# A hybrid decoder step on one core: sample attention started two pairs earlier, both lead-ins reordered, out-projection products moved ahead of the last values

## What is computed

```python
# layer 0: h @ w_in -> q, k, v, xq
o  = softmax(q k^T * hd**-0.5 - slopes*dist, with a sink per head) v   # window 128, 12 heads, 4 kv heads
xo = softmax(xq mk^T * hd**-0.5) mv                                    # 4 heads into 256 memory tokens
x  = x + concat([o, xo]) @ w_out
# layer 1: o = u * (tril(W_s) v_norm + b) in chunks of 128; xo and x as in layer 0
# samples: the same with cached keys and values, 8 batches of 4 tokens
```

## Time and profile before

| | us |
|---|---|
| median of 3 runs | 2238.39 (2238.03 to 2239.85) |
| the profiled execution | 2238.22 |
| its span, first to last instruction | 2236.3 |
| PE busy in the span | 2216.7 |
| DVE, ACT, POOL busy | 1174.1, 664.5, 553.2 |
| mean granted TensorE clock | 0.999 of full speed |

### The profile page before, as it was taken

The page is one execution under the profiler, slowest core; times in us unless marked ns, Lnnn a source line. Parts: engine busy times, 40 slices in busy tenths (PEclk is TensorE's granted clock), DMA queues, the critical chain, the costliest instruction groups (busy, mean ns, idle before and its releaser), DMA issues.

```text
span 2236.3 us, 39236 instructions
## 1 busy us (share of the span) xinstructions
PE 2216.7 (99%) x15320; PEld 2142.0 (96%) x15320; DVE 1174.1 (53%) x2164; ACT 664.5 (30%) x1208; POOL 553.2 (25%) x422
## 2 busy tenths in 40 slices
PE   9999999999999999999999999999999999999999
PEld 8997689999999999999999997999999999999999
DVE  8355761745545455444575256165545455454554
ACT  6314962512221122221253226142221122221121
POOL 0004634312221122221252223332221122221221
PEclk9999999999999999999999999999999999999999
DMA  5223001111111011110111130111111111110112
GB/s 189 82 97 141 13 18 43 57 39 47 56 56 34 32 47 56 56 38 29 49 49 61 47 109 18 47 38 57 57 49 37 37 47 56 56 38 28 47 57 91
DMA packets 39305, 123.43 MB, mean 55 GB/s; under 512 B 5328, under 2 KB 13488, under 8 KB 38416
## 3 DMA queue, kind: packets, MB, share of 16 engines
q1 hardware_dynamic: 36384, 113.25, 15.3%
q10 hardware_dynamic: 2832, 8.94, 1.1%
HBM read 115.57 MB, written 8.63 MB: 56 GB/s over the span
## 4 chain that ended last, share of the span: by engine, by line
PE 93%; DVE 3%; ACT 2%; issue 1%; POOL 1%; DMA 0%; SPq 0%; DVEq 0%; ACTq 0%; POOLq 0%
PE ps L634 29%; PE ps L635 29%; PE ps L636 29%; DVE h_lo L1743 2%; ACT s_exp L1437 1%; PE ps L982 1%; PE ps L1027 1%; PE ps L1008 1%; PE ps L815 1%; PE ps L951 1%; ACT p_t L1222 0%; PE ps L803 0%; PE ps L770 0%; DMA x<-in_x_t 0%; PE ps L954 0%
## 5 line engine op out<-in xcount | busy, mean ns | idle before, releaser
L634 PE MATMUL ps<-h_hi,w_hi 128*128 128x352 f32 x3120 | 1013.3, 325 | 4.6 <-DVE h_lo L1743 4.4
L635 PE MATMUL ps<-h_lo,w_hi 128*128 128x352 f32 x3120 | 1000.9, 321 | 0.0
L636 PE MATMUL ps<-h_hi,w_lo 128*128 128x352 f32 x3120 | 1000.4, 321 | 0.0
L486 POOL TENSOR_TENSOR w_lo<-raw,w_hi 128x1024 fp32r<-128x1024 f32 x118 | 298.5, 2530 | 1497.0 <-ACT w_hi L1222 1497.0
L634 PEld LDWEIGHTS ps<-h_hi,w_hi 128*128 128x128 f32 x3120 | 585.8, 188 | 17.2 <-issue 6.2
L635 PEld LDWEIGHTS ps<-h_lo,w_hi 128*128 128x128 f32 x3120 | 586.9, 188 | 0.7
L636 PEld LDWEIGHTS ps<-h_hi,w_lo 128*128 128x128 f32 x3120 | 585.4, 188 | 0.0
L2160 DVE TENSOR_TENSOR x<-x,ps 128x352 f32<-128x352 f32 x528 | 270.8, 520 | 170.5 <-PE ps L636 169.8
L634 PE MATMUL ps<-g_hi,d_hi 128*128 128x352 f32 x1056 | 340.2, 322 | 0.0
L635 PE MATMUL ps<-g_lo,d_hi 128*128 128x352 f32 x1056 | 339.9, 322 | 0.0
L636 PE MATMUL ps<-g_hi,d_lo 128*128 128x352 f32 x1056 | 339.7, 322 | 0.0
(11 more groups left out here) (204 smaller groups left out, 1691.6 us busy)
## 6 DMA issues: line engine op xcount, KB each, us to landing
raw<-in_w SPq DMA_DIRECT2D x181, 512.0 KB, 3.7
s_mk<-in_s_mk SPq DMA_DIRECT2D x2, 2048.0 KB, 9.6
s_mv<-in_s_mv SPq DMA_DIRECT2D x2, 2048.0 KB, 14.4
out_y<-x ACTq DMA_DIRECT2D x7, 528.0 KB
x<-in_x_t SPq DMA_DIRECT2D x2, 1408.0 KB, 11.8
mem_x<-in_mem_t SPq DMA_DIRECT2D x1, 1024.0 KB, 9.0
s_k<-in_s_k SPq DMA_DIRECT2D x2, 512.0 KB, 5.0
s_v<-in_s_v SPq DMA_DIRECT2D x1, 1024.0 KB, 16.2
```

Of the source, the lines that this page charges most:

```text
L486: pool.tensor_tensor(lo, raw[:, slot], hi.bitcast(F32), ALU.subtract).then_inc(prepped, 1)
L634: pe.matmul(out, a, hi_x(k), start=(first and n == 0), stop=False)
L635: pe.matmul(out, a, lo_x(k), start=False, stop=False)
L636: ins = pe.matmul(out, b, hi_x(k), start=False, stop=(last and n == len(ks) - 1))
```

## The change

Layer 0, lead-in: on ACT `exps(1)` moves ahead of the first copy of turned values; in pair 2 PE makes `turn_sample_rows` and the values of items 0 and 1 between scores(4) and scores(5), and ACT copies the sample rows between exps(4) and exps(5). Layer 1, lead-in: the first `scale` moves into the gate's last step on DVE; all memory scores of the samples move from pair 0 to between scores(2) and scores(3).

Sample steps: step 0 of layer 0 is at pair 6 instead of 8. Window turn, new turn and memory turn are at offsets 11, 12 and 13 instead of 12, 13 and 14 (pairs 17, 18 and 19 instead of 20, 21 and 22), POOL's norms stay at offsets 10 and 11 (pairs 16 and 17 instead of 18 and 19). The values are made in 8 steps (pairs 20 to 27) instead of 5 (pairs 23 to 27). First and last outputs stay in pairs 28 and 30. In layer 1 the steps are spread over pairs 1 to 7 instead of 0 to 5, and from pair 2 on they stand ahead of the values.

Tail: `AHEAD` is 4 instead of 2; `first_outputs` is made in two parts of two k each, at pair M and at pair M+1, both after the turns and ahead of the values. ACT's and DVE's first seven pieces are laid 2, 3 and 2 into pairs M-1, M and M+1 instead of 4 and 3 into M and M+1.

```diff
-SAMPLE_AT = (8, 0)
+SAMPLE_AT = (6, 0)
...
-             8: ("memory scores", 1, 0), 9: ("memory scores", 1, 1), 12: ("window turn",), 13: ("new turn",),
-             14: ("memory turn",), 15: ("window values", 0), 16: ("window values", 1), 17: ("window values", 2),
-             18: ("memory values", 0), 19: ("memory values", 1), 20: ("first outputs",), 22: ("last outputs",)},
-            {0: ("all memory scores",), 3: ("memory turn",), 4: ("all memory values",), 5: ("last outputs",)})
...
+             8: ("memory scores", 1, 0), 9: ("memory scores", 1, 1), 11: ("window turn",), 12: ("new turn",),
+             13: ("memory turn",), 14: ("values", 0), 15: ("values", 1), 16: ("values", 2), 17: ("values", 3),
+             18: ("values", 4), 19: ("values", 5), 20: ("values", 6), 21: ("values", 7), 22: ("first outputs",),
+             24: ("last outputs",)},
+            {1: ("all memory scores",), 5: ("memory turn",), 6: ("all memory values",), 7: ("last outputs",)})
+ACT_STEPS = ({7: ("window exp", 0), 8: ("window exp", 2), 10: ("memory exp",), 11: ("window turn",), 12: ("new turn",),
+              13: ("memory turn",), 16: ("window values",), 21: ("memory values",)},
+             {2: ("memory exp",), 5: ("memory turn",), 6: ("memory values",)})
...
+              22: ("outputs", 0), 23: ("outputs", 2), 24: ("outputs", 4), 25: ("outputs", 6)},
+             {2: ("memory top",), 3: ("memory sums",), 7: ("outputs", 6)})
+POOL_STEPS = ({10: ("window norm",), 11: ("memory norm",)}, {3: ("memory norm",)})
+AHEAD = 4
+
+
+def cuts_at(layer, it):
+
+    return {-1: (0, 1), 0: (2, 3, 4), 1: (5, 6)}.get(it - len(item_pairs(layer)), ())
...
+                    if a == 0:
+                        new_values(0)
+                        window_values(0, 0)
+                    if a == 1:
+                        window_values(0, 1)
+                        new_values(1)
                     if a == 2:
...
+                        window_values(1, 0)
+                        window_values(1, 1).then_inc(m["s_pv"], 1)
+                    if a == 3:
+                        new_values(2)
+                        window_values(2, 0)
+                    if a == 4:
+                        window_values(2, 1)
+                        memory_values(0, 0)
+                    if a == 5:
+                        memory_values(0, 1)
+                    if a == 6:
+                        memory_values(1, 0)
+                    if a == 7:
+                        memory_values(1, 1).then_inc(m["s_pv"], 1)
...
-                    if it == M + 1:
-                        first_outputs()
+                    if it >= M:
+                        first_outputs(it - M)
+                    if l == 0 and it == 2:
+                        turn_sample_rows()
+                        values(0)
+                        values(1)
+                    if l == 1 and it == 1:
+                        sample_step(l, *step_of(PE_STEPS, l, it))
...
                     exps(0)
+                    exps(1)
                     take_values(0)
-                    exps(1)
...
                         if q == NB:
                             top(1)
+                            scale(0)
                         multiply(q, w)
...
-                    if 1 <= it <= M:
+                    if 1 <= it <= M and (l == 0 or it > 1):
                         scale(2 * it - 2)
```

More of the change, by code:

```diff
@@ L144 @@
-ACT_STEPS = ({7: ("window exp", 0), 8: ("window exp", 2), 10: ("memory exp",), 12: ("window turn",), 13: ("new turn",),
-              14: ("memory turn",), 16: ("window values",), 19: ("memory values",)},
-             {1: ("memory exp",), 3: ("memory turn",), 4: ("memory values",)})
+             8: ("memory scores", 1, 0), 9: ("memory scores", 1, 1), 11: ("window turn",), 12: ("new turn",),
+             13: ("memory turn",), 14: ("values", 0), 15: ("values", 1), 16: ("values", 2), 17: ("values", 3),
@@ L869, in sample_step, with window_values @@
                     mm.then_inc(m["s_turned"], 1)
-                def window_values(j, at):
-                    out = ps[:, 7, at:at + 256]
-                    pe.matmul(out, sp_new[:, j, :], v_tok[0:TS, NB, :], start=True, stop=False, skip_group_check=True)
-                    return in_groups(out, sp_pad[:, j, :], lambda b: s_v[:, b, :], False, True, skip=True)
-                def memory_values(kc):
+                def window_values(j, par):
+                    return in_groups(ps[:, 7, 256 * (j % 2):256 * (j % 2) + 256], sp_pad[:, j, :], lambda e: s_v[:, e, :],
+                                     False, True, skip=True, halves=(par,))
@@ L877, in memory_values, with new_values @@
+                def new_values(j):
+                    return pe.matmul(ps[:, 7, 256 * (j % 2):256 * (j % 2) + 256], sp_new[:, j, :], v_tok[0:TS, NB, :],
+                                     start=True, stop=False, skip_group_check=True)
+                def memory_values(kc, par):
                     return in_groups(ps[:, 7, 256:512], sp_pad[:, 3 + kc, :], lambda e: s_mv[l][:, kc, e, :],
-                                     kc == 0, kc == 1)
-                if step == "window values":
+                                     kc == 0, kc == 1, halves=(par,))
@@ L892, in sample_step @@
                 if step == "all memory values":
                     pe.wait_ge(m["s_turned_taken"], 1)
-                    memory_values(0)
-                    memory_values(1).then_inc(m["s_pv"], 1)
+                    for kc in range(2):
+                        for par in range(2):
+                            mm = memory_values(kc, par)
+                    mm.then_inc(m["s_pv"], 1)
                 if step == "first outputs":
@@ L1497, in prompt_attention @@
                     sample_step(l, *step_of(ACT_STEPS, l, it))
-                    if it >= M:
-                        for e in range(4 * (it - M), min(4 * (it - M) + 4, 7)):
-                            cut(e)
+                    for e in cuts_at(l, it):
+                        cut(e)
                 for e in range(7, KD * NCH):
@@ L2064, in prompt_attention @@
                     sample_step(l, *step_of(DVE_STEPS, l, it))
-                    if it >= M:
-                        for e in range(4 * (it - M), min(4 * (it - M) + 4, 7)):
-                            low(e)
+                    for e in cuts_at(l, it):
+                        low(e)
                 for e in range(7, KD * NCH):
```

39 lines of the change are left out of this document (14 added, 25 removed).

## The result

The changed kernel takes 2245.89 us (median of 8 executions, 2244.85 to 2247.56) against 2238.96 us of the kernel before (8 executions beside them). The ratio is 1.003, 95% interval 1.0022 to 1.0039: slower by 6.9 us, 0.3%, which is beyond the 0.2% that a measurement can tell. The profiled execution took 2244.85 us, of which 2242.7 are its span; before it was 2238.22 and 2236.3.

A forecast was written before the change was run, and what follows sets the result against it. TensorE, busy 2216.7 of 2236.3 us, was taken as the bound, so only its attention-stage idle time could change. Terms 0.0 - 0.6 + 3.0 + 0.5 + 0.55 - 0.8 = +2.65 us on 2238.22 gave 2240.9 us, range 2237.0 to 2243.5.

The forecast's parts named there:

- The stall: Pair 17 of layer 0: PE waits 3.1 us for POOL's normalised window rows before transposing them; bounds 2.3 and 3.6.
- Lead-in of layer 0: Part 1: PE's 1.50 us wait is filled, but POOL's queue holds turn(5) at 210.49; 0.0 us, bounds -0.5 and +0.2.
- Sample steps two pairs earlier: Part 2, pairs 6 and 7: sample scores laid over the ring's slack, stretched transposes lose their excess; -0.6 us.
- Window transposes: Part 3, pair 17: one pair closer to POOL's normalising; 3.1 stall plus 1.13 minus 1.2 of other waits, +3.0 us.
- Parts 1 to 4: Layer 0's lead-in, earlier sample steps, window transposes and split values: 0.0, -0.6, +3.0 and +0.5 us.
- Values in pieces: Part 4, from pair 20: three more group changes cost 0.4 us and a first piece ahead of ACT 0.1; +0.5 us.
- bare pairs: Prompt pairs where PE has no sample work between scores and values and waits for ACT's copy, 0.63 us in pair 19.
- Tail of layer 0: Part 5: six more out-projection products ahead of the values; first wait 1.5 us, not 1.07; +0.55 us, bounds -1.3 and +1.0.
- Layer 1: Part 6: the 0.82 us wait of the memory transposes goes, the tail gives 0.4 back; -0.8 us, bounds -1.8 and 0.
- rival A: PE's clock falls at the stall, costing 1.6 us: 2242.5 us, or 2244.1 with a second slow stretch; chance 0.31.
- A's second half: A second slow-clock stretch follows in the small matmuls of pairs 17 and 18: 3.2 us, 2244.1 us; chance 0.09.
- part 5: Layer 0's tail, six more out-projection products ahead of the values: +0.55 us; layer 1's like tail gives 0.4 back.

The follow-up runs named there:

- e6: Kernel before with only the new lead-in of layer 0 (ACT order, sample turns and values(0), (1) ahead of scores(5)); 2238.74 us, ratio 1.0003.
- e10: e3 with POOL's second bias moved from pair 1 to pair 4 and its clearing of sp_pad to pair 5; single execution 2235.22 us.
- e5: Changed kernel with nine unused identity products on PE ahead of the wait for the window rows; 2243.65 us, ratio 1.0022.
- e1: Changed kernel with window rows normalised one pair earlier on POOL (pair 15), DVE's window sums and memory top exchanged; 2240.48 us, ratio 1.0007.
- e9: e3 with the samples' values again in five steps in pairs 23 to 27; single execution 2238.38 us.
- e3: Changed kernel with the edits of e1 and e2 together (earlier window normalising, old tail); 2237.78 us, ratio 0.9991.
- e11: e3 with the edits of e9 and e10 together; 2237.13 us, ratio 0.9989.
- e2: Changed kernel with the tail of both layers as before (AHEAD 2, rounding and first products as before); 2242.16 us, ratio 1.0014.
- e8: Kernel before with AHEAD 4 instead of 2 and nothing else; 2238.51 us, ratio 0.9998.
- e7: e1 with DVE's low(0) and low(1) moved behind the last pair's reciprocals in both layers' tails; 2239.44 us, ratio 1.0002.
- e4: Kernel before with only the window transposes and their copy one pair earlier (pair 19), POOL's normalising left in pair 18; 2241.87 us, ratio 1.0011.
- e12: The kernel of e10 again, for its time; 2236.11 us, ratio 0.9986.

## Why the prediction failed, point by point

The forecast was 2240.9 us with a range to 2243.5, and the time is 2245.89. The stall, its cause and its length were there as walked. Two steps failed. The sum put the granted clock behind the waits at 1.00, that is at no cost, and it lost 2.16 us in the trace. And the new tail was priced at 0.55 us in layer 0 and 0.4 in layer 1, and costs 1.65 and 1.63 at the full clock, 2.33 more. With other terms of -0.74 that makes the 3.75 us by which the sum missed the 6.40 in the traces. Neither alone would have left the range: 2240.9 with the one is 2243.1, with the other 2243.2. In the order of its parts:

1. **Lead-in of layer 0, 0.0: right.** turn(5) stands at 14.01 us after the first scores against 14.08, held by POOL's queue; e6 shows it alone, e10 that the hold is POOL's.
2. **Sample steps two pairs earlier, -0.6: right.** The first window scores of the prompt come 26.84 us after the first scores before and 27.50 after, 0.66 later with two sample steps of 0.68 more done: -0.70, of which 0.07 is the lead-in. The stretched transposes of the earlier trace rows are at their short form, in the timeline of PE of after:

```profile
218.96 0.71 PE L1036 MATMUL ps<-ident,s_exp 64*128 64x64 f32 x16
...
222.33 0.71 PE L1036 MATMUL ps<-ident,s_exp 64*128 64x64 f32 x16
```

3. **Window transposes, +3.0: the wait right (3.23 for 3.1), its price a little high.** e5 less e1 is 2.80 for the stall at the full clock. Parts 1 to 4 together were to give 2.9 without the clock and gave 103.25 - 100.93 = 2.32. Of the 0.6 between them 0.3 is the stall's price, and the other 0.3 stands under 4.
4. **Values in pieces, +0.5: wrong in sign.** Small pieces laid from pair 20 on save 0.76 us (e9 against e3, and e11 against e10). I priced three group changes (0.4) and forgot what the prediction itself says of bare pairs: without sample work PE waits for ACT's copy, as the earlier trace rows shows. The error was half hidden by its opposite: with whole steps and no stall I had A to B at -0.6 + 1.13 - 1.2 = -0.67, and e9 shows 101.20 - 100.93 = +0.27, because moving the chain ahead leaves pairs 20 to 22 bare. So -0.67 + 0.5 = -0.17 was forecast and +0.27 - 0.76 = -0.49 came (e3).
5. **Tail of layer 0, +0.55: 1.65 at the full clock.** The first wait came nearly as walked (1.63 for 1.5). What was mis-sized is the second: turn(63) was to wait 0.1 and waits 0.62 (e1), because POOL's four normalisings began behind DVE's low parts and took 2.72 us, not the 1.84 of before, so everything behind them came later. These two make 0.65 of the 1.10 us missed; the rest lies in small pieces on the way to the last k, and no run splits it. e2 confirms the tail as the place (2.35 and 1.63), e8 clears the added products, e7 takes 0.77 of it back by DVE's order in layer 1.
6. **Layer 1, -0.8: its middle right, its tail not.** e2 shows -1.24 without the new tail, where -1.2 was worked out; the tail took 1.63, not 0.4. In all +0.39.
7. **The clock: left at 1.00, and rival A had only 0.31.** In the trace it fell at both long waits. The first fall cost 1.48 us (e5), close to A's 1.6, and every execution has it. The second was not where A's second half had it, in the small matmuls just behind the stall (the clock is back at 1.00 over 260 to 270), but at the tail's 1.63 us, for 0.68 us; that one is a matter of the single trace, since e1 and e3 have the same clocks. The start of the trace had shown a fall after a wait of 1.72 us and one of 0.68, and I weighed that too little against the 1.50 us of the earlier trace rows at which it held.

The Trainium skill ("TensorE: Matmul & The Clock Gate", section "Why this matters for your kernels") warns of long idle gaps between bursts, and the trace agrees at the 3.23 us. The waits at which the clock fell otherwise (1.72 us at the start, with which the prediction had it agree, and 1.63 in the tail) are shorter than those that the section speaks of, so it covers the first fall alone. Had I priced rival A in, the sum would have been 2242.5, which is still too low.

The range was too narrow on the slow side because the ends of the single terms (tail 1.0 in one layer, clock 1.6) were never added up: part 5 was priced once per layer with two different small numbers, though both tails have the same order of work. Adding them (0.2 for the lead-in, 0.5 for the stall, 0.45 for the tail, 0.8 for layer 1 and 1.6 of clock) gives about 2244.5, nearer but still under what was measured, since both tails lie beyond their own ends.

Left open: what decides whether the clock falls at waits of 1.6 to 1.7 us. It fell at 1.63 (after) and 1.70 (e7) and held at 1.64 (e1) and 1.63 (e5). Left open too is what e7 gains in layer 0 beyond the estimate above, and how the tail's loss divides between ACT's rounding and DVE's low parts.

## What to carry to other kernels

Before a step is moved nearer to the one that feeds it, find in which of its own iterations the feeding engine reaches it and what else stands in that iteration: POOL lagged a pair behind PE here, and one bias made 2.3 us into 3.2. Price a long wait on PE together with the clock it may lose (1.48 us beside 2.80 here), and add up the worst ends of the terms once before giving a range. Spare work spread in small pieces over the iterations that would wait was worth more here than the group changes it cost (0.76 us), and work put ahead of a queue's reciprocal or copy must be priced by who stands behind it.

## What was new of the hardware

**POOL and DVE hold each other up.** All normalisings of 128x256 in the lines table (count, then shortest, median and longest ns, first and last start, forms), first of the kernel before, then of after:

```profile
L570 POOL TENSOR_SCALAR s_exp<-s_exp,stat x160: 371/478/505, 199.6 to 1379.5; 128x256 f32<-128x256 f32 x148, 128x128 f32<-128x128 f32 x12
```

```profile
L578 POOL TENSOR_SCALAR s_exp<-s_exp,stat x160: 371/478/1098, 198.7 to 1387.0; 128x256 f32<-128x256 f32 x148, 128x128 f32<-128x128 f32 x12
```

The longest went from 505 to 1098 ns. That one is in layer 1's lead-in, where the change put scale(0) ahead of a multiplication with two inputs in SBUF (timeline of after); the same four took 1.84 us before:

```profile
1359.54 0.94 DVE L2054 TENSOR_TENSOR z<-mixed,z 128x768 f32<-128x768 f32 x1
...
1359.73 2.46 POOL L578 TENSOR_SCALAR s_exp<-s_exp,stat 128x256 f32<-128x256 f32 x4 [21.11 <-DVE stat L2020]
```

In the tail of layer 0 of after, the lines table cut to 308.3 to 309.2 us has for POOL and, cut to 307.7 to 308.1 and to 308.6 to 309.3, for DVE:

```profile
L578 POOL TENSOR_SCALAR s_exp<-s_exp,stat x2: 738/916/1095, 308.1 to 309.1; 128x256 f32<-128x256 f32 x2
...
L2034 DVE TENSOR_TENSOR h_lo<-z,h_hi x1: 699/699/699, 307.8 to 307.8; 128x352 fp32r<-128x352 f32 x1
...
L2034 DVE TENSOR_TENSOR h_lo<-z,h_hi x2: 514/612/710, 308.4 to 308.8; 128x352 fp32r<-128x352 f32 x2
```

A low part that meets a running normalising takes 699 and 710 ns instead of 518 (before, the longest of 48 was 539), and a normalising that meets a low part takes 1095 and 738 instead of 478. So each seems to wait for the other's running instruction rather than to share with it. The Trainium skill ("SBUF — State Buffer", section "SBUF: two separate sides") states just that for a DVE operation with two inputs in SBUF against an operation of GpSimd (POOL) that reads SBUF, and the numbers agree. It is a rule that speaks against this change, and the prediction didn't weigh it: before, the first low part began only 0.18 us ahead of the end of POOL's last normalising (304.12 against 302.46 + 1.84 = 304.30), and it is the longest of the 48; the change laid three low parts over the four normalisings. How much of the tail's 1.1 us beyond the forecast is this (0.88 us on POOL) and how much the later start no run parts cleanly. e7 starts the normalisings earlier and keeps most of the overlap (four in 2.45 and 2.46 us, where e1 has 2.72), and it gives 0.77 us back in layer 1, of which the shorter POOL time (0.27) can explain a third and the earlier start the rest.

**The clock fell at a wait inside dense work of small matmuls.** 3.23 and 3.24 us brought it to 0.83 over the ten us around (after, e2), and no execution of these two kernels has a mean above 0.998; 2.27 (e4) didn't in the trace. It cost 1.48 us the one time it was taken away alone.

**The clock also falls where PE hardly waits, and that makes a large part of the scatter of this kernel.** In six of the fourteen traces (e2, e3, e4, e5, e9, e12) it fell between 1328 and 1340 us, in the small matmuls of layer 1's gate, where PE waits 0.58 or 0.59 us ahead of them in all fourteen and not otherwise between 1322 and 1345. C to D takes 1040.42 to 1041.02 us in these six and 1038.84 to 1039.60 in the other eight. In four (before, e3, e8, e11) it fell at the kernel's start. The 31 executions of the kernel before in the series of e1 to e4 took 2237.85 us in the mean at a granted clock of 1.000, 2239.44 at 0.999 and 2241.24 at 0.998, 1.6 to 1.8 us for each step. What decides whether it falls there is not shown by any run.
